# Reordered norms, gates and first weights in a two-block transformer stack on one core

## What is computed

```python
def short_conv_mixer(h, w_in, w_conv, w_out):
    gate_b, gate_c, xin = jnp.split(h @ w_in, 3, axis=-1)
    y = gate_b * causal_depthwise_conv(gate_c * xin, w_conv)
    return y @ w_out

# state-space mixer: decay and angle per state, then a scan over tokens
mag = jnp.exp(a_re * dt); ab_re = mag * jnp.cos(a_im * dt); ab_im = mag * jnp.sin(a_im * dt)
bu_re = jnp.einsum('bsgh,gph->bsgp', ug, bb_re)
_, _, x_re, x_im = lax.associative_scan(combine, (la_re, la_im, bu_re, bu_im), axis=1)
y = einsum(x_re, c_re) - einsum(x_im, c_im) + d_skip * ug

# sparse attention: queries and gates from one projection
qg = u @ w_qg
gates = jax.nn.sigmoid(qg[..., N_HEADS * HEAD_DIM:].reshape(..., N_BRANCH))
o = gates[..., 0:1] * o_cmp + gates[..., 1:2] * o_slc + gates[..., 2:3] * o_win
return o.reshape(bsz, seq, D_MODEL) @ w_o
```

## Time and profile before

| | us |
|---|---|
| median of three runs (lowest, highest) | 1919.35 (1918.03, 1920.93) |
| the profiled execution | 1921.98 |
| its span, first to last instruction | 1920.1 |
| PE busy, with its share | 1860.1 (97%) |
| DVE, ACT, POOL busy | 1284.7, 927.2, 635.5 |
| mean granted clock of PE | 0.987 of 2.4 GHz |

### The profile page before, as it was taken

How to read it: one execution, slowest core, us unless ns; L and a number is a source line. 1 busy time by engine, 2 the same in 40 slices (tenths; PEclk the granted TensorE clock), 3 DMA queues, 4 the chain that set the end, 5 groups by cost and what they waited for, 6 DMA issues and landing times.

```text
span 1920.1 us, 31815 instructions
## 1 busy us (share of the span) xinstructions
PE 1860.1 (97%) x13410; PEld 1716.7 (89%) x13427; DVE 1284.7 (67%) x1503; ACT 927.2 (48%) x1214; POOL 635.5 (33%) x756
## 2 busy tenths in 40 slices
PE   8999999899999999999999989999999999999999
PEld 6979999899999899988997878998989989778998
DVE  6878666666664777677666756666656665657665
ACT  4354445444334554455444245444654454755443
POOL 6968880476753887010001620000000002420000
PEclk9999999999999999999999899999999998999999
DMA  6555564454444566557556315665355642015553
GB/s 243 187 186 214 214 215 181 151 187 165 155 165 144 172 216 215 209 194 289 193 181 214 116 73 205 220 219 182 137 169 193 211 179 88 23 39 181 189 184 110
DMA packets 54954, 336.35 MB, mean 175 GB/s; under 512 B 7915, under 2 KB 13084, under 8 KB 17948
## 3 DMA queue, kind: packets, MB, share of 16 engines
q1 hardware_dynamic: 45648, 297.51, 43.1%
q10 hardware_dynamic: 5068, 22.13, 3.0%
q0 software_dynamic: 4096, 14.68, 2.2%
HBM read 318.54 MB, written 15.75 MB: 174 GB/s over the span
## 4 chain that ended last, share of the span: by engine, by line
PE 84%; DVE 9%; ACT 4%; issue 2%; POOL 1%; ACTq 0%; DVEq 0%; POOLq 0%
PE psum L507 22%; PE psum L460 13%; PE psum L461 13%; PE psum L462 13%; PE psum L509 11%; DVE w_lo L1952 3%; ACT w_hi L1152 2%; DVE both L1959 1%; ACT both L1152 1%; PE psum L935 1%; PE psum L973 1%; PE psum L1093 1%; PE psum L1062 1%; DVE h L1965 1%; PE psum L923 1%
## 5 line engine op out<-in xcount | busy, mean ns | idle before, releaser
L1952 DVE TENSOR_TENSOR w_lo<-raw,w_hi 128x2048 fp32r<-128x2048 f32 x277 | 653.4, 2361 | 200.9 <-ACT w_hi L1152 198.1
L507 PE MATMUL psum<-both,w_hi 128*128 128x512 f32 x1984 | 702.7, 397 | 9.6 <-DVE both L1959 6.8
L1152 ACT ACTIVATE w_hi<-raw 128x2048 fp32r<-128x2048 f32 x280 | 534.1, 1909 | 179.7 <-PE psum L462 178.2
L509 PE MATMUL psum<-both,w_lo 128*128 128x256 f32 x1984 | 556.6, 281 | 0.0
L460 PE MATMUL psum<-both,w_hi 128*128 128x256 f32 x1600 | 464.2, 290 | 16.4 <-DVE both L1959 10.0
L507 PEld LDWEIGHTS psum<-both,w_hi 128*128 128x128 f32 x1984 | 372.7, 188 | 98.0 <-DVE both L1959 7.9
L461 PE MATMUL psum<-both,w_hi 128*128 128x256 f32 x1600 | 454.9, 284 | 0.0
L462 PE MATMUL psum<-both,w_lo 128*128 128x256 f32 x1600 | 454.8, 284 | 0.0
L509 PEld LDWEIGHTS psum<-both,w_lo 128*128 128x128 f32 x1984 | 375.5, 189 | 0.1
L460 PEld LDWEIGHTS psum<-both,w_hi 128*128 128x128 f32 x1600 | 308.6, 193 | 17.1 <-DVE both L1959 11.6
L461 PEld LDWEIGHTS psum<-both,w_hi 128*128 128x128 f32 x1600 | 308.8, 193 | 0.8 <-issue 0.2
(11 more groups left out here) (402 smaller groups left out, 2504.4 us busy)
## 6 DMA issues: line engine op xcount, KB each, us to landing
raw<-in_weights SPq DMA_DIRECT2D x280, 1024.0 KB, 4.8
table<-tables ACTq DMA_DIRECT2D x8, 1792.0 KB, 8.5
tables<-st POOLq DMA_DIRECT2D x16, 512.0 KB, 4.3
tables<-st POOLq DMA_DIRECT2D x8, 256.0 KB, 5.8
tables<-turns POOLq DMA_DIRECT2D x8, 256.0 KB, 4.4
w<-in_cmp_w ACTq DMA_DIRECT2D x4, 512.0 KB, 5.2
tbl<-in_cmp_w ACTq DMA_DIRECT2D x4, 512.0 KB, 5.2
tbl<-bias_v SPq DMA_DIRECT2D x128, 16.0 KB, 4.7
```

Of the source, the lines that this page charges most:

```text
L507: nc.tensor.matmul(bank, wh[:, cols], both[x][:, c].rearrange("p e t -> p (e t)"), start=c == 0, stop=False, skip_group_check=True)
L509: return nc.tensor.matmul(bank[:, 0:SEQ], wl[:, cols], x_hi[x][:, c], start=False, stop=c == KC - 1, skip_group_check=True)
L1152: copy = lambda out, in_, **kw: nc.scalar.activation(out, in_, ACT.Copy, **kw)
L1952: tt(w_lo[:, g % RING], raw[:, g % RING], w_hi[:, g % RING].bitcast(F32), ALU.subtract).then_inc(sem["lo_ready"], 1)
```

## The change

In the program of each engine:
- First weights: SP loads the second unit before the constants and the third only once the second has landed; ACT interleaves squares and roundings; DVE splits the first activation pair and first weights at once. The 31 chained operations go behind convolution triple 0 (13) and triple 1 (18), ACT's Abs and two Sin behind triple 1. POOL's program isn't changed.
- Rotary angles: steps 2 and 3 of four go behind the last activation pair.
- State-space stage: DVE multiplies `h` with the gain alone, before the norm is there; the copies into `u2` follow, and `u2` is multiplied in place with the norm (eight operations), which ACT copies out by token phase. PE has 10 zero products around the norm's broadcast instead of 30, 14 new ones before the first outputs and 5 before each of the last two. The split of the last weights of `ffn0` (which rounds and subtracts unit glu + 2) goes behind the copies on ACT and behind the last scan on DVE.
- Gates: the weights (48 wide) are stationary and 256 tokens move, ACT copies the result, PE turns it by two transposes.
- Third projection unit: its chunks are multiplied during the last heads (`third_rows`).

```diff
@@ -337,6 +337,7 @@
         q_squares = [ta, tb]
+        gate_rows = tc[0:3 * NH, 0, :]
         def q_total(u):
@@ -418,7 +419,9 @@
                     sp.wait_ge(sem["h_landed"], 16 * PAIRS)
+                if u == 1:
                     sp.dma_start(con[:], A["con"]).then_inc(sem["con_landed"], 16)
+                    sp.wait_ge(raw_landed[1], 16)
             bias_v = A["bias_v"].tensor
@@ -903,18 +906,16 @@
             norm_sum(R_FFN0)
+            clear_sums()
+            keep_warm(4, XB)
+            norm_bcast(R_FFN0)
             keep_warm(6, XB)
-            norm_bcast(R_FFN0)
-            keep_warm(24, XB)
-            clear_sums()
             def states(c):
...
                 pe.wait_ge(table_landed[c % TSLOTS], 16 * (c // TSLOTS + 1))
-                for name in ("u2_dve", "u2_act", "u2_pool"):
-                    pe.wait_ge(sem[name], c // 4 + 1)
+                pe.wait_ge(sem["u2_dve"], 2 + c + 1)
                 w_ = table[c % TSLOTS][:, T_W:T_T].rearrange("p (j r s) -> p j r s", j=JJ, r=2)
@@ -942,9 +943,16 @@
                 last.then_inc(sem["y_turned"], 1)
+            def add_zeros(n, bank):
+                for _ in range(n):
+                    nc.tensor.matmul(bank, zero[:, 0:P], zero[:], start=False, stop=False, skip_group_check=True)
             for c in range(3):
                 states(c)
+            add_zeros(14, DB[0])
             for c in range(KC):
+                if c >= KC - 2:
+                    add_zeros(5, DB[3])
                 outputs(c)
@@ -1028,13 +1036,18 @@
             pe.wait_ge(sem["wg_lo_ready"], 1)
-            for t in range(TT):
-                for c in range(KC):
-                    last = exact(DB[0][:, t * 64:t * 64 + 3 * NH],
-                                 tuple(xx[x][:, c, t * P:(t + 1) * P] for xx in (x_hi, x_lo)),
-                                 (wg_hi[:, c, :], wg_lo[:, c, :]), c == 0, c == KC - 1)
+            for c in range(KC):
+                last = exact(DB[0][0:3 * NH, 0:SEQ], (wg_hi[:, c, :], wg_lo[:, c, :]), (x_hi[x][:, c], x_lo[x][:, c]),
+                             c == 0, c == KC - 1)
             last.then_inc(sem["gate_done"], 1)
             norm_bcast(n)
+            def turn_gates():
+                pe.wait_ge(sem["gate_sig"], 1)
+                for t in range(TT):
+                    last = nc.tensor.transpose(DB[1][:, t * 64:t * 64 + 3 * NH], gate_rows[:, t * P:(t + 1) * P],
+                                               ident[0:3 * NH, 0:3 * NH])
+                last.then_inc(sem["gate_done"], 1)
             def q_sums(u):
@@ -1109,8 +1122,22 @@
                         last.then_inc(sem["unit_done"], 1)
-            up_unit(g_q + 1, 0, x, q_bank[1], mid=lambda: q_sums(0))
-            pe.wait_ge(sem["gate_sig"], 1)
+            def third_rows(c0, c1):
+                if c0 == 0:
+                    pe.wait_ge(sem["lo_ready"], g + 3)
+                    pe.wait_ge(sem["n_log"], NH)
+                    nc.tensor.matmul(DB[0], zero[:, 0:P], zero[:], start=True, stop=False, skip_group_check=True)
+                pe.wait_ge(sem["n_lo"], c1)
+                for c in range(c0, c1):
+                    for q in range(2):
+                        last = exact(DB[0][:, q * SEQ:(q + 1) * SEQ], wide(slot(g + 2), c, q),
+                                     (x_hi[0][:, c], x_lo[0][:, c]), False, c == KC - 1)
+                if c1 == KC:
+                    last.then_inc(sem["unit_done"], 1)
+            up_unit(g_q + 1, 0, x, q_bank[1], mid=lambda: (turn_gates(), q_sums(0)))
+            pe.wait_ge(sem["gate_sig"], 2)
             n_scores(0)
@@ -1126,6 +1153,8 @@
                                          skip_group_check=True)
+                if step >= NH - 1:
+                    third_rows(*((0, 2), (2, 4), (4, 5))[step - NH + 1])
                 if step >= 2:
@@ -1133,16 +1162,9 @@
             out_part(KC - 2)
-            pe.wait_ge(sem["lo_ready"], g + 3)
-            pe.wait_ge(sem["n_log"], NH)
-            nc.tensor.matmul(DB[0], zero[:, 0:P], zero[:], start=True, stop=False, skip_group_check=True)
-            for c in range(KC):
-                if c == 2:
-                    out_part(KC - 1)
-                for q in range(2):
-                    last = exact(DB[0][:, q * SEQ:(q + 1) * SEQ], wide(slot(g + 2), c, q),
-                                 (x_hi[0][:, c], x_lo[0][:, c]), False, c == KC - 1)
-            last.then_inc(sem["unit_done"], 1)
+            third_rows(5, 7)
+            out_part(KC - 1)
+            third_rows(7, 8)
             up_unit(g + 3, 0, 0, DB[1])
@@ -1321,7 +1343,8 @@
                         residual(r, m, x)
-                split(g + 3 * FFN_PAIRS - 1)
+                if f:
+                    split(g + 3 * FFN_PAIRS - 1)
             def ple(l, n, r):
@@ -1352,18 +1375,11 @@
                 x_high(R_IN, m)
-            for m in range(PAIRS):
-                squares(R_IN, m)
             for g in range(1, RING):
+                squares(R_IN, 2 * g - 2)
+                squares(R_IN, 2 * g - 1)
                 act.wait_ge(raw_landed[g], 16)
                 copy(w_hi[:, g], raw[:, g]).then_inc(sem["hi_ready"], 1)
-            act.wait_ge(sem["sm_dve"], S5_R)
-            act_fn(sm[:, 8], sm[:, 5], ACT.Abs).then_inc(sem["sm_act"], 1)
-            act_fn(e_one[:, :, 1], sm[:, 5], ACT.Sin).then_inc(sem["sm_act"], 1)
-            act.wait_ge(sem["sm_act"], 3)
-            act.wait_ge(sem["fill_done"], 4)
-            act_fn(e_one[:, :, 0], sm[:, 8], ACT.Sin, scale=-1.0, bias=halfpi[:]).then_inc(sem["sm_act"], 1)
             def conv_triple(g0, k, j):
@@ -1376,7 +1392,15 @@
             conv_triple(0, 0, 0)
-            for k in range(0, PAIRS - 1):
+            conv_triple(3, 0, 1)
+            act.wait_ge(sem["sm_dve"], S5_R)
+            act_fn(sm[:, 8], sm[:, 5], ACT.Abs).then_inc(sem["sm_act"], 1)
+            act_fn(e_one[:, :, 1], sm[:, 5], ACT.Sin).then_inc(sem["sm_act"], 1)
+            act.wait_ge(sem["sm_act"], 3)
+            act.wait_ge(sem["fill_done"], 4)
+            act_fn(e_one[:, :, 0], sm[:, 8], ACT.Sin, scale=-1.0, bias=halfpi[:]).then_inc(sem["sm_act"], 1)
+            for k in range(1, PAIRS - 1):
                 conv_triple(3, k, k + 1)
@@ -1493,7 +1517,6 @@
             load_table(4)
-            norm(R_FFN0)
             def move(half):
@@ -1516,6 +1539,12 @@
             move(1)
+            act.wait_ge(sem["bcast_ready"], R_FFN0 + 1)
+            steps = norm_bank(R_FFN0)[:, SEQ:2 * SEQ].rearrange("p (k i) -> p i k", i=SL)
+            for i in range(SL):
+                last = copy(rs[32 * i:32 * i + 32, 0, 0:SK], steps[32 * i:32 * i + 32, i])
+            last.then_inc(sem["rs_ready"], 1)
+            split(BASE["glu"] - 1)
             act.wait_ge(sem["u2_dve"], 2)
@@ -1618,10 +1647,12 @@
             q_copy(0)
+            act.wait_ge(sem["gate_done"], 1)
+            copy(gate_rows, DB[0][0:3 * NH, 0:SEQ]).then_inc(sem["gate_sig"], 1)
             split(g)
-            act.wait_ge(sem["gate_done"], 1)
+            act.wait_ge(sem["gate_done"], 2)
             for t in range(TT):
-                last = act_fn(gate[:, t], DB[0][:, t * 64:t * 64 + 3 * NH], ACT.Sigmoid, scale=rs_tok[:, t:t + 1])
+                last = act_fn(gate[:, t], DB[1][:, t * 64:t * 64 + 3 * NH], ACT.Sigmoid, scale=rs_tok[:, t:t + 1])
             last.then_inc(sem["gate_sig"], 1)
@@ -2192,44 +2224,22 @@
                         split(g + 1 + m)
-                    if l == 0:
+                    if l == 0 and m < 2:
                         angles(m)
                 x_low(r, PAIRS - 1)
+                if l == 0:
+                    angles(2)
+                    angles(3)
                 split(g + PAIRS)
-            dve.wait_ge(sem["sm_act"], 1)
-            link(tt(sm[:, 1], are, sm[:, 0], ALU.mult))
...
-            link(dve.reciprocal(sm[:, 12], sm[:, 11]))
-            assert count[0] == S5_R
             def first_split(g):
...
                 tt(w_lo[:, g], raw[:, g], w_hi[:, g].bitcast(F32), ALU.subtract).then_inc(sem["lo_ready"], 1)
-            for m in range(2):
-                x_low(R_IN, m)
+            x_low(R_IN, 0)
             first_split(0)
-            for m in range(2, PAIRS):
+            for m in range(1, PAIRS):
                 x_low(R_IN, m)
@@ -2273,7 +2283,30 @@
             conv_triple(0, 0, 0)
-            for k in range(0, PAIRS - 1):
+            dve.wait_ge(sem["sm_act"], 1)
+            link(tt(sm[:, 1], are, sm[:, 0], ALU.mult))
+            link(ts(sm[:, 1], sm[:, 1], 2.0 ** -S5_HALVINGS, None, ALU.mult))
+            link(dve.tensor_copy(sm[:, 2], sm[:, 1]))
+            for n in (6, 5, 4, 3, 2):
+                link(ts(sm[:, 2], sm[:, 2], 1.0 / n, 1.0, ALU.mult, ALU.add))
+                link(tt(sm[:, 2], sm[:, 2], sm[:, 1], ALU.mult))
+            conv_triple(3, 0, 1)
+            for _ in range(S5_HALVINGS):
+                link(stt(sm[:, 2], sm[:, 2], 2.0, sm[:, 2], ALU.add, ALU.mult))
...
```

(39 more changed lines are left out.)

29 lines of the change are left out of this document (11 added, 18 removed).

## The result

The changed kernel takes **1929.97 us** (1928.3 to 1931.49, five runs) against 1919.35 before: ratio 1.0053, 95% interval 1.0039 to 1.0068. It is slower by half a per cent, 10 us above the forecast and 2 us outside the range. The profiled execution took 1930.52 us with a span of 1928.7, 8.5 us above that of before (1921.98). That is 7.9 us more than the sum of the terms (+0.6). The other 2.1 us of the miss are the step from a profiled execution to the median: it was 2.63 us before and only 0.55 in the kernel after, a difference between executions that no term of the sum is to blame for.

A forecast was written before the change was run, and what follows sets the result against it. TensorE, busy 1860.1 of 1920.1 us, was taken as the bound. Terms +21.1 - 2.0 - 10.5 - 8.3 + 0.3 = +0.6 on the profiled 1921.98, less 2.63, gave 1920.0 us; range 1913 to 1928.

The forecast's parts named there:

- The angle chain and POOL's queue: Kernel start: moved chain makes POOL's `input_matrices` late, holding the squares' adds of norm R_SC; +21.1 us, ends +17 and +25.
- the 15 to 20 that I named as a sign: Sign of being right: a PE wait of 15 to 20 us before the seventh chunk of the first MLP unit.
- Start: Kernel start: PE begins 3.6 us earlier, first norm's sum 1.5 us earlier, a gain that does not reach the end.
- Angles, gates, third unit: Rotary angle steps moved, -2.0 us; last attention's gates with tokens moving, -8.3; third projection unit during the heads, +0.3.
- the two ends: Gates of the last attention: -8.3 us if the clock holds, -4 if it falls; the upper value was taken.
- State-space stage: Earlier recurrence and zero products holding the clock shorten this stage by 10.5 us; ends -5 and -12.5.
- First outputs at 1065.5: State-space stage: states end at 1062.5, fillers take 3.0 us, then PE begins the first outputs at 1065.5.
- shows holding for the two-input subtractions only: State-space stage: one-input gains and copies would not hold POOL's adds of squares; otherwise the norm comes up to 2.7 us later.
- POOL's 4.1 to 5.0 us a step decides: State-space stage after the first outputs: POOL sets the pace, its last step ends at 1100.5, the last outputs at 1102.5.
- the last outputs may stay slow: End of the state-space stage: the second filler (5 and 5) is short against the 2.85 us wait; outputs priced at 1.9.
- The clock falls anyway: Rival, 0.18: clock drops in the state-space stage (5.5 us lost) or gates (4.3 lost); 1924.3 with one, 1929.8 with both.
- POOL is later still: Rival, 0.11: DVE's other operations also hold POOL at the kernel's start, its run ends 3 to 5 us later; 1924.

The follow-up runs named there:

- The last run: Changed kernel with the angle chain back at the start, the subtraction behind the third gated-activation subtraction, 8 zero products instead of 14 before the first outputs: 1901.7 us.

## Why the prediction was wrong

**The angle chain and POOL's queue: right.** POOL's run was to start at 70.0 and started at 68.03; it was to end at 138.4 and ended at 135.10; the broadcast was to come at 150.4 and came at 149.09. The term was +21.1 and is +19.7, inside its ends, in part by luck: the run ended 3.3 us early, and the way from there to the broadcast took 14.0 us where I had 12.0. PE's wait was 12.4 us and not the 15 to 20 that I named as a sign. The chain of waits is in the trace, and the run with the chain back at the start takes it away. What I did not see is that PE has a second wait on the same run, at the first table's products; here it lies behind the first and costs nothing, but it forbids the obvious mend.

**Start: right that it does not count, too small by itself.** The first norm's copy came 3.2 us sooner (30.15 to 26.93) and the first triple 4.6 (44.31 to 39.67) where I took 1.5; POOL's run swallowed all of it. With the chain spread, a kernel in which that run is not late, the earlier start is used up before the norm R_SC as well.

**Angles, gates, third unit: right.** -1.8, -8.0 and +0.6 against -2.0, -8.3 and +0.3. The first is the weakest: from the norm's copy ahead of it to the one behind it the kernel before took 33.9 us and the kernel after 32.1, but two other kernels with the old order (state-space part alone, gates alone) took 33.0 and 32.9, so the edit's own share is between 0.8 and 1.8. The clock held in the gates at 1.00; the value between the two ends was the right one.

**State-space stage: wrong, and by far the largest error.** The step that failed is "POOL's 4.1 to 5.0 us a step decides", and with it the 1.9 us for the last outputs. With this term as predicted the median would have been some 8 us lower, inside the range; without the 2.1 us between profiled execution and median it would just have been inside as well (1927.9). My steps put the end of the last outputs 59.4 us behind the last residual add (1102.5 less 1043.12), 11.6 us sooner than before, of which I took 10.5. They ended after 65.2. Step by step:
- "First outputs at 1065.5", 22.4 us behind the add: measured 24.3. The in-place multiplies let the states begin after 12.35 us, and with 3.0 us each they end after 21.2, where I had 19.4. DVE's own start was right (14.2 against 14.7); I had let PE run ahead of the multiplies it reads. They begin only 11.7 us behind the add. Two causes are in the trace: the variance came 1.7 us behind PE's sum instead of 1.0, standing behind the second four gains on DVE; and POOL's adds of the squares (1062.92 to 1066.05) lie beside DVE's first copies. The six copies took 3.83 us, with 1.24 and 1.39 for the two beside the adds and 0.28 for each of the other four; the second six took 2.70:

```profile
1063.55 3.83 DVE L2418 COPY u<-u 32x256 f32<-32x256 f32 x6
...
1070.17 2.70 DVE L2418 COPY u<-u 32x256 f32<-32x256 f32 x6
```

  The prediction's reading that the trace "shows holding for the two-input subtractions only" does not carry over to this kernel: these copies have one input.
- "POOL's 4.1 to 5.0 us a step decides": in the changed kernel DVE decides, with 5.24. The prediction has a price for PE and for POOL in a step and none for DVE, whose operations add up to 3.5 us at the lengths they have beside an idle POOL; the lengths beside a busy POOL stood in the last step of the kernel before and were not used. The last run has POOL's pace, 4.94, and ends POOL's last step after 57.7 us without the subtraction; mine was 57.4 with two microseconds of subtraction in it. From the first step's end (23.2) that leaves 4.6 us a step, 0.3 too few even for POOL alone.
- The subtraction on POOL's last step was priced at 2 us. It costs 2.4, and with it PE's wait is 4.08 us instead of 1.77: "the last outputs may stay slow" was written down, but only 1.9 us were put into the sum for them. The half clock costs 3.5 us, in the outputs and behind them, and that was a term left out.
- 1.6 us more went behind the stage. In both kernels PE waits 1.5 us ahead of the next `ffn`, and its clock is low behind that; the windows from there on show it low for some 3 us in the kernel before,

```profile
1148.00:1150.00 2.00, 2.00 (x7) 1.40 (x6) 1.77 (x2) 1.37 (x2) 0.15 (x1) 0.51 0.66 221
1150.00:1152.00 2.00, 2.00 (x10) 1.71 (x9) 1.37 (x3) 0.00 (x0) 0.56 (x1) 0.64 1.04 405
```

and for over 6 in the kernel after:

```profile
1162.00:1164.00 2.00, 2.00 (x5) 0.89 (x4) 2.00 (x2) 1.72 (x2) 0.00 (x0) 0.53 0.71 156
1164.00:1166.00 2.00, 2.00 (x8) 1.71 (x7) 1.15 (x5) 0.00 (x0) 0.71 (x1) 0.50 0.97 388
1166.00:1168.00 2.00, 2.00 (x7) 1.71 (x7) 2.00 (x1) 0.00 (x0) 0.00 (x0) 0.50 1.10 443
```

The runs with one part each fall on either side of this (from the gated unit's copy to the norm 31.9 us with the state-space part alone, 33.5 with the gates alone), with nothing edited there, and the other traces have the one or the other too: it is luck of one execution's clock, and no reason of the change.

Together: -11.6 + 5.9 (outputs end later than thought) + 1.9 (half clock behind them) + 1.6 = -2.2, in this pair of executions. The part alone gave 3.7 us by the medians of the whole time (1.5 to 5): that is the better number for what the stage is worth, and it too is far from 10.5.

**The rivals.** "The clock falls anyway" put the slower case at 1924.3 to 1929.8 and held 0.18: it came nearest to the time, though its upper end lay outside my own range of 1913 to 1928, and its place was wrong. The clock held in both places that it named and fell at the last outputs, which stood only as a half-sentence. "POOL is later still" was wrong at the start of the kernel, but its mechanism, DVE operations other than the large subtraction meeting POOL, is what the state-space stage shows.

## What to carry to other kernels

When a chain is moved down its engine's program, follow each of its readers through that reader's whole queue, and then look for the second reader of the same result: here POOL's tables were read by the norm and by TensorE. Where two engines pass work back and forth, put both into the sum, with the lengths of their operations from a stretch where both work, and ask which of them will have no gap: POOL alone gave 4.6 us a step where 5.24 were measured with VectorE. Before a stage is priced against one trace, look at the same unchanged stage in another: here its end varied by 4.4 us. A large operation with no deadline belongs where nobody it meets is awaited: the same subtraction cost 5.9 us in the traces (3.9 by the medians) beside the last step of a chain, and nothing that could be seen three operations later.

## What the runs showed of the hardware

POOL and VectorE slow each other, in both directions: VectorE's sum of 128x512 takes 0.69 us alone and 1.24 beside POOL, its two scans 1.27 and 2.52, while its products with one side in PSUM keep their length (0.66 to 0.69 and 0.41 us). Operations with one input are stretched as well: a gain of 128x256 took 1.10 us beside POOL's adds and 0.45 later, a copy of 32x256 1.39 and 0.28. POOL's operation of 128x512 takes 1.28 us and, beside a subtraction of 128x2048, 3.24. A stationary tile of 48 columns runs 256 moving columns every 0.12 us, as 128 do. TensorE's clock was low behind each wait of 4.08 us, of 3.50 and of 2.85 ahead of the last outputs behind none of 1.77 or less there and not behind one of 2.41 ahead of the seventh outputs (gates alone), but also behind the one of 1.5 us ahead of the next `ffn`, and behind one of three waits of 2.16 us ahead of the first outputs: the length of the wait alone does not tell. Nor does it tell how long the clock stays low: behind two waits of 4.2 us ahead of the first outputs it was some 3 us in one execution and some 12 in another.
